# A third product unit beside the first two after each norm, square sums over all partitions, and first modulation loads in halves, in a two-layer decoder step

## What is computed

```python
def rmsnorm(x, g):
    y = x * rsqrt(mean(x * x, axis=-1) + EPS)
    return y * g
def modulated_norm(x, g, shift, scale):
    return rmsnorm(x, g) * (1 + scale) + shift
def half_ffn(x, mod, g, w_up, w_down):
    h = modulated_norm(x, g, mod[0], mod[1])
    a, b = split(h @ w_up, 2)
    return x + 0.5 * mod[2] * ((silu(a) * b) @ w_down)
# layer: half_ffn; h = modulated_norm(x); z = h @ W_in; three mixers; x += gate * W_out(...); half_ffn
```

## Time and profile before

| | us |
|---|---|
| median of three runs (3161.19 to 3166.5) | 3165.66 |
| the profiled execution | 3163.12 |
| its span, first to last instruction | 3161.5 |
| PE busy (share of the span) | 3097.9 (98%) |
| DVE, ACT, POOL busy | 1190.1, 840.8, 138.5 |
| mean granted share of the TensorE clock | 0.991 |
| DMA moved | 390.00 MB, 123 GB/s over the span |

### The profile page before, as it was taken

The page is one execution under the profiler, slowest core; times in us unless marked ns, Lnnn a source line. Parts: engine busy times, 40 slices in busy tenths (PEclk is TensorE's granted clock), DMA queues, the critical chain, the costliest instruction groups (busy, mean ns, idle before and its releaser), DMA issues. The chain is left out here.

```text
span 3161.5 us, 54219 instructions
## 1 busy us (share of the span) xinstructions
PE 3097.9 (98%) x23440; PEld 2765.0 (87%) x23440; DVE 1190.1 (38%) x2091; ACT 840.8 (27%) x1281; POOL 138.5 (4%) x269
## 2 busy tenths in 40 slices
PE   8999999999999999999999999999999999999999
PEld 6999998877777899999999999988776878899999
DVE  4333334344432344333353323442534223533333
ACT  3221224332321123212232212242324212322121
POOL 0000000000411000000000000000003120000000
PEclk9999999999999999999999999999999999999999
DMA  6444442111358432333223444312022682322212
GB/s 237 150 173 158 160 145 84 68 54 37 100 175 268 137 122 101 133 141 116 85 83 136 170 172 150 125 62 94 29 75 65 215 289 91 116 81 87 101 71 79
DMA packets 119047, 390.00 MB, mean 123 GB/s; under 512 B 12828, under 2 KB 63356, under 8 KB 100504
## 3 DMA queue, kind: packets, MB, share of 16 engines
q1 hardware_dynamic: 100608, 338.36, 30.1%
q0 software_dynamic: 14432, 34.09, 3.1%
q10 hardware_dynamic: 3768, 14.08, 1.1%
HBM read 372.79 MB, written 13.69 MB: 122 GB/s over the span
## 5 line engine op out<-in xcount | busy, mean ns | idle before, releaser
L1621 ACT ACTIVATE w_hi<-w 128x1024 fp32r<-128x1024 f32 (+2 forms) x232 | 266.0, 1147 | 1229.4 <-PE g L868 905.0
L868 PE MATMUL g<-h_hi,w_hi 128*128 128x272 f32 x2688 | 561.0, 290 | 8.4 <-ACT area L1631 4.5
L868 PE MATMUL g<-h_hi,w_lo 128*128 128x272 f32 x2688 | 556.6, 288 | 0.0
L868 PE MATMUL g<-h_lo,w_hi 128*128 128x272 f32 x2688 | 553.5, 287 | 0.0
L2200 DVE TENSOR_TENSOR w_lo<-w,w_hi 128x1024 fp32r<-128x1024 f32 (+2 forms) x232 | 309.5, 1336 | 496.0 <-ACT w_hi L1621 493.0
L868 PEld LDWEIGHTS g<-h_hi,w_hi 128*128 128x128 f32 x2688 | 422.0, 189 | 27.2 <-ACT area L1631 16.3
L868 PEld LDWEIGHTS g<-h_lo,w_hi 128*128 128x128 f32 x2688 | 421.0, 188 | 0.0
L868 PEld LDWEIGHTS g<-h_hi,w_lo 128*128 128x128 f32 x2688 | 420.4, 188 | 0.0
L868 PE MATMUL g<-h_hi,w_rest 128*128 128x272 f32 x1280 | 370.2, 289 | 0.0
L868 PE MATMUL g<-acts_hi,w_hi 128*128 128x272 f32 x1408 | 305.7, 291 | 0.1
L868 PE MATMUL g<-acts_hi,w_lo 128*128 128x272 f32 x1408 | 301.2, 288 | 0.0
(11 more groups left out here) (308 smaller groups left out, 4248.9 us busy)
## 6 DMA issues: line engine op xcount, KB each, us to landing
w<-in_w_up SPq DMA_DIRECT2D x43, 2048.0 KB, 7.8
w<-in_w_ada SPq DMA_DIRECT2D x32, 2048.0 KB, 7.9
w<-in_w_in SPq DMA_DIRECT2D x16, 2048.0 KB, 8.1
w<-in_w_down SPq DMA_DIRECT2D x16, 1536.0 KB, 6.9
w<-in_w_gate SPq DMA_DIRECT2D x48, 512.0 KB, 5.6
w<-in_w_down SPq DMA_DIRECT2D x16, 1280.0 KB, 5.7
area<-in_cache_k SPq DMA_DIRECT2D x72, 256.0 KB, 3.9
area<-in_cache_v SPq DMA_DIRECT2D x72, 256.0 KB, 4.5
```

The lines of the kernel that those rows point to most:

```text
L868: return pe.matmul(o, a, b, start=start, stop=stop, skip_group_check=True, **kw)
L1621: ac.activation(WH[i % 2][:, 0:n], W[place][:, o:o + n], ACT.Copy).then_inc(s_wh, 1)
```

## The change

- **A third unit.** From norm 1 on the third unit of the next product joins the first two (`first_units`, `first_together`). Its blocks stand in a row behind those of the first two: after block 7 of half 0 its eight blocks of half 0, and after block 7 of half 1 its eight blocks of half 1. Its result goes to the two banks `Q`, which the modulation vectors use at other times, and ACT reads it there.
- **Its weights.** Three pieces (for `ua` all four) are split ahead of the norm, at blocks 4 and 5 of the product before it, or, after the mixers, at block 5. The pieces split inside an FFN's norm are now those of units 3 and 4, and the Silu table is loaded behind block 13 of `hi_of_h`. First weights have a semaphore of their own (`s_wf`).
- **Sums on all partitions.** A half's squares are summed in four strips of 68 columns on 128 partitions, and root, reciprocal and spread work on 128 x 68. The sum for half 0 stands one block earlier in `last_pair`, that for half 1 one block later in `first_units`, and so do the spreads.
- **First loads.** Each of the pieces 1 to 3 of `w_ada` is loaded in two halves, one from SP and one from ACT. `vectors(3)` follows `vectors(2)` directly; ACT copies both rows behind block 4, and splits the two next weight pieces behind blocks 9 and 10 and loads the Silu table behind block 13.

```diff
-QT = T // 4
+QH = HALF // 4
...
+def first_together(n):
+    return 2 if n == 0 else 3
...
-        RS4, _ = take(QT, start=o_d)
+        RS4, _ = take(2, QH, start=o_d)
-        SUMS = [TB[64 * h:64 * h + 64, h, 300:300 + QT] for h in range(2)]
+        SUMS = [TB[:, h, 300:300 + QH] for h in range(2)]
...
-            sp.dma_start(WA[2], d["w_ada"][ADA_ORDER[2][1]]).then_inc(s_first[2], 16)
-            sp.wait_ge(s_first[2], 16)
+            for i in range(1, FIRST_ADA):
+                sp.dma_start(WA[i][:, 0:SLOT // 2], d["w_ada"][ADA_ORDER[i][1]][:, 0:SLOT // 2]).then_inc(s_first[i], 16)
+            sp.wait_ge(s_first[FIRST_ADA - 1], 32)
...
-                    for j in (2 * h, 2 * h + 1):
-                        last = mm(TB[32 * j:32 * j + 32, h, 300:300 + QT], ones[:, 0:32], H[:, k, j * QT:(j + 1) * QT],
+                    for j in range(4):
+                        o = h * HALF + j * QH
+                        last = mm(SUMS[h][32 * j:32 * j + 32], ones[:, 0:32], H[:, k, o:o + QH], k == 0, k == KD - 1)
...
-                mm(TB[:, h, 0:HALF], ones[r], RS[r, h * HALF:(h + 1) * HALF], True, True).then_inc(s_rs, 1)
+                mm(TB[:, h, 0:HALF], ones, RS[:, h * HALF:(h + 1) * HALF], True, True).then_inc(s_rs, 1)
...
-                            if (h, r, k) == (1, 0, 3):
+                            if (h, r, k) == (1, 0, 2):
                                 norm_sum(KD - 1, 0, (0,))
-                            if (h, r, k) == (1, 0, 7):
+                            if (h, r, k) == (1, 0, 6):
                                 spread_roots(n, 0)
...
-                    if n and q == 1:
+                    if n and q == 2:
                         norm_sum(KD - 1, 0, (1,))
-                    if n and q == 4:
+                    if n and q == 5:
                         spread_roots(n, 1)
+                    if n and k == KD - 1:
+                        for k3 in range(KD):
+                            block(2, h, k3)
+                if n:
+                    un.take()
...
-                ac.activation(RS4[r], SUMS[h], ACT.Sqrt, bias=EPSC[r, 2:3], scale=1024.0 / D).then_inc(s_rms, 1)
+                ac.activation(RS4[:, h], SUMS[h], ACT.Sqrt, bias=EPSC[:, 2:3], scale=1024.0 / D).then_inc(s_rms, 1)
...
+                    if split and q in (10, 12):
+                        split()
+                    if table and q == 13:
+                        table()
...
+                        if norm_next and m >= PAIR - 2:
+                            begin, end = ((0, 2), (2, 4 if f == 0 else 3))[m - PAIR + 2]
+                            if f == 0:
+                                hi_part(l, *[("ua", i) for i in range(begin, end)])
+                            else:
+                                first_hi(l + 1, 0, range(begin, end))
...
-            for i in range(1, FIRST_ADA, 2):
-                ac.dma_start(WA[i], d["w_ada"][ADA_ORDER[i][1]]).then_inc(s_first[i], 16)
+            for i in range(1, FIRST_ADA):
+                ac.dma_start(WA[i][:, SLOT // 2:], d["w_ada"][ADA_ORDER[i][1]][:, SLOT // 2:]).then_inc(s_first[i], 16)
...
-                link(ve.reciprocal(RS4[r], RS4[r]))
+                link(ve.reciprocal(RS4[:, h], RS4[:, h]))
```

More of the change, by code:

```diff
@@ L732, in release @@
                     splits.n += FFN_UNITS[what[2]]
+                    if what[2] == 0:
+                        together = first_together(3 * what[0] + 2 * what[1])
+                        splits.n -= together
+                        firsts.n += together
+                        sp.wait_ge(s_wf, firsts.value())
                     units.n += FFN_UNITS[what[2]]
@@ L1565, in first_norm @@
                 rows(1)
-                for q in range(KD + 1):
-                    if q == KD:
-                        rows(3)
+                for q in range(2 * KD):
                     hi_of_h(0, q)
@@ L1571, in first_norm, with norm @@
                         samples_hi(slice(0, 4))
-                    if q == 5:
+                    if q == 4:
                         rows(2)
-                for q in range(KD + 1, 2 * KD):
-                    hi_of_h(0, q)
+                        rows(3)
                     if q == 11:
                         samples_hi(slice(4, 8))
-                ac.wait_ge(s_w[0], LANDED[0])
-            def norm(n, then):
+                    if q in (9, 10):
+                        if q == 9:
+                            ac.wait_ge(s_w[0], LANDED[0])
+                        then()
+                    if q == 13:
+                        silu_table()
+            def norm(n, split=None, table=None):
                 first, second = slice(0, HALF), slice(HALF, T)
@@ L1646, in ffn @@
                     for c in range(blocks):
-                        chunk(c, half == c == 0)
+                        third = (half, c) == (0, 1) and at[0] > 4
+                        chunk(c, not half == c == 0 and not third, not half == c == 0, Q[:, :, 0:HALF] if third else None)
                         if c % 2 == 1:
@@ L1734, in _ @@
                 ffn(l, 0)
-                norm(3 * l + 1, lambda i: hi_part(l, ("ua", 2 + i)))
-                each(4, lambda i, p: ac.activation(halves(YA[:, i, :]), both(p), ACT.Gelu_apprx_tanh,
+                norm(3 * l + 1)
+                each(4, lambda i, p: ac.activation(halves(YA[:, i, :]), Q[:, :, 0:HALF] if i == 2 else both(p),
+                                                   ACT.Gelu_apprx_tanh,
                                                    bias=ZERO[:, 0:1]), l, {i: [("va", i)] for i in range(4)})
@@ L2231, in ffn @@
                     for c in range(blocks):
-                        chunk(c, c, half == c == 0)
+                        third = (half, c) == (0, 1) and at[0] > 4
+                        chunk(c, c, not half == c == 0 and not third, not half == c == 0)
                         turn_over()
@@ L2242, in ffn @@
                         turn_over()
+                        if half == 1 and norm_follows(l, f) and m >= PAIR - 2:
+                            weights_ahead(m - PAIR + 2)
                         if m % 2 == 1:
@@ L2282, in add_to_x @@
                         lo_part(l, ("out", 4 + m))
-                norm(3 * l + 2, gate, lambda r: first_lo(l, 1, r))
+                    if m == PAIR - 1:
+                        for i in range(3):
+                            first_lo(l, 1, i)
+                norm(3 * l + 2, gate, lambda nth: None)
             ve.memset(EPSC[:, 0:1], EPS)
@@ L2304, in _ @@
                 ffn(l, 0)
-                lo_part(l, ("ua", 2), ("ua", 3), *[("va", i) for i in range(4)], ("rows", 0))
+                lo_part(l, *[("va", i) for i in range(4)], ("rows", 0))
                 wait(small, 9)
```

114 lines of the change are left out of this document (55 added, 59 removed).

## The result

The changed kernel takes **3135.15 us** (median of 4 runs, 3131.3 to 3137.5). The kernel before, run beside it, takes 3163.44 (4 runs, 3161.19 to 3166.5). The ratio is 0.9909 with a 95% interval of 0.9892 to 0.9926: 28 us less, or 23 to 34. The prediction said faster, 3145.4, with a range of 3139 to 3156.

The account below looks back on a forecast made before the run. PE, busy 98% of the span, was taken as the bound. Norms -16.8, start -1.75 and clock -1.7 gave -20.3 us from the profiled 3163.12, so 3142.9; with 2.5 more for the median, 3145.4, range 3139 to 3156.

Parts of the forecast that it names:

- PE's waits in the norms cost their full length: Norms 1 to 5: PE's 26 waits, 15.4 us, cost 19.6 with overlap; 2.8 stay, so 16.8 us less.
- I take 0: Square sums: 16 instructions of half the columns for 8 cost nothing more; one half's sum may save 0.1 a norm.
- the rival by instruction: Square sums: each instruction costs 0.055 us, so 384 more cost 21 us and the gain is gone, 3166; chance 0.06.
- The floor of 25 ns a start: Square sums: matmul starts never come closer than about 25 ns, so 384 more cost 9.6 us, 3155.
- The spread over 272 columns stays as it is: Norms' chain of roots: spreading the reciprocals costs PE the same as before, so no gain was counted.
- Its idle time and about 0.16 more: PE's waits: each costs its idle time plus about 0.16 us of lost overlap between matmuls.
- Hidden weight work, landings at block 4: Products ahead of norms: earlier weight splits fit into idle time and loads land in time; price nothing.
- the slower rival: Block 4: ACT waits for late weights, holding up DVE and PE in norms 1, 3 and 4; 3172, chance 0.03.
- given back: Behind the norms: PE meets its next waits for weights or pages earlier and stands there; 3160 to 3166, chance 0.04.
- Piece 1, 2.0 us: Start: half loads on two queues remove PE's wait of 1.86 + 0.16 us for piece 1 of the first weights.
- Norm 0 behind block 0: Start: 0.2 given back by block 8, 1.1 of stretched second half, 1.65 less wait ahead of the third unit.
- The clock: Behind the wait ahead of norm 0's third unit: clock stays at 2.4 GHz, 1.7 us less, ends 0 and 1.7.

Follow-up runs that it names:

- third_behind: Changed kernel with the third unit whole behind block 15 of the first two units, PE's order alone edited: 3145.2 us, ratio 0.9946 to the kernel before.
- spread_rows: Kernel before with only the spread of the reciprocals reading 128 rows, 64 of them zeros: 3161.43 us, ratio 0.9998 to the kernel before.
- third_old_sums: Changed kernel with sums, roots, reciprocals and spreads in the old form (64 partitions for a half), at the changed places: 3137.98 us, ratio 0.993.
- loads_only: Kernel before with the first vectors' loads in halves and the new order of norm 0 alone: 3157.82 us, ratio 0.9984.
- halves_only: Kernel before with pieces 1 to 3 of w_ada loaded in two halves alone, norm 0's order as before: 3156.88 us, ratio 0.9986.
- table_behind: Changed kernel with the Silu table load of norms 2, 3 and 5 put back behind the last block of h: 3130.62 us, ratio 0.9899.
- table_all_warm: Changed kernel with the Silu table behind the last block of h in norm 0 too, plus two more products of zeros: 3131.5 us, ratio 0.9895.
- warm_more: Changed kernel with two more products of zeros at its start (26 for 24): 3136.18 us, ratio 0.9912 to the kernel before.

## Why the prediction was right in sign and too small

Of the 10.3 us between 3145.4 and 3135.15, the norms make 5.0, the start 2.6 and the rest of the program -2.2. The other 4.9 are of the step from the profiled execution to the median: I added 2.5, as in the three runs of before, but the changed kernel's median lies 2.35 below its profiled execution. So this step failed by the chance of single executions. Without it the forecast of 3142.9 against 3137.5 is still 5.4 too slow, by these steps:

- **PE's waits in the norms cost their full length.** Right. 19.6 us were forecast as lost, 2.8 of them to stay. What stayed is 4.5, with the overlap of 0.16: the table 2.4 (2.2 forecast), 1.3 in norm 1 ahead of block 6, and 0.4 ahead of block 6 in norms 2 and 5 each. third_behind shows that the third unit's place does it.
- **"I take 0" for the sums.** This is a step that failed, though its first half held: the sum of both halves has 16 instructions and takes what 8 took, 0.44, and the rival by instruction is out:

```profile
468.28 0.44 PE L880 MATMUL tb<-h,cst 128*32 128x68 f32 x16
468.65 0.40 PE L880 MATMUL g<-acts_hi,w_hi 128*128 128x272 f32 x1
```

  The floor of 25 ns a start, cited from the Trainium skill, "TensorE: Matmul & The Clock Gate", section "Wait — 56ns, not 53.3ns?", does not hold for strips side by side: 16 of them take 0.37 us to the next matmul, 23 ns each, and the four strips of a set start 7 ns apart. But a sum of one half is 0.1 us cheaper, and there are four such savings in a norm, not the one that I allowed at the lower end: 3.51 us of sums in a norm became 3.13, 0.38 each, 1.9 in five norms.
- **"The spread over 272 columns stays as it is."** Of the norms' terms this and the sums above, both put at nothing, failed most. A spread over 128 rows is 0.2 us cheaper for half 0, and 0.3 for half 1 where it now stands (in norm 4 from 2039.52 to 2040.10, 0.58 for 0.88): 2.5 in five norms. For norm 0 I even charged 0.6 for its two spreads, where (25.03 - 24.11) - (26.35 - 25.69) = 0.26 was lost. I looked at the columns and not at the rows of the tile. The Trainium skill, "TensorEngine Tiling (Array Packing)", section "Key Properties", says that a change of tiling mode drains the engine. The spread over 64 rows was such a change and the new one is not. The rows agree (0.65 to 0.36 in spread_rows, with nothing else changed on PE; and where PE has not waited ahead of it, the step into the spread is 0.22 us over 64 rows, in norm 3 of third_old_sums, and 0.13 over 128, in the same place of the changed kernel), though they do not show that the drain is the reason.
- **"Its idle time and about 0.16 more."** Mis-sized, as a wait costs a slow step behind it too: the second matmul starts 0.20 to 0.23 us after the first, for 0.125. A block of h that comes just in time has such steps with no wait in the profile, as block 13 in norm 2 of the kernel before:

```profile
1204.15 0.29 PE L868 MATMUL g<-h_hi,w_rest 128*128 128x272 f32 x1
1204.38 0.39 PE L868 MATMUL g<-h_hi,w_hi_middle 128*128 128x272 f32 x1
1204.61 0.28 PE L868 MATMUL g<-h_lo,w_hi_middle 128*128 128x272 f32 x1
```

  There were five such steps in norm 2 (three of them behind a wait) and there is one now; over the five stretches, sums and spreads left out, 26 of them lost 2.8 us and 3 lose 0.3, so 2.5 less. The prediction added up waits and could not see it.
- Together: 19.6 + 1.9 + 2.5 + 2.5 - 4.5 = 22.0, for 21.8 found.
- **Hidden weight work, landings at block 4.** Right: no wait at the end of a product ahead of a norm, so neither the slower rival nor "given back" took place.
- **Piece 1, 2.0 us.** Right: from the row behind the spreads, here as it was before, to `vectors(1)` at 29.39 it was 3.0 us; 25.03 to 26.04 is 2.0 less.

```profile
26.35 1.18 PE L868 MATMUL g<-cst 128*128 128x272 f32 x4
```

- **Norm 0 behind block 0.** The net forecast, 0.2 + 1.1 - 1.65 = -0.35, failed in both halves. Block 8 came 1.9 earlier against block 0 and not 0.2 later, since with both vectors together the wait ahead of it is 0.48 for 1.91; and from there to the third unit it is 0.7 longer, not 0.55 shorter. Net -1.2; loads_only against halves_only gives 1.3.
- **The clock.** The fall at 61 us was priced at 1.7, and from the third unit to the first turned vectors 1.5 were won. The fall at 20 us was not in the sum, and its absence in the profiled execution made 1.3. This was not foreseen, and it does not come in every execution: two of the nine profiles with the new loads have the fall. With it the start would stand at -4.8, and the profiled pair at 24.3 less, 3138.8 in place of 3137.5.

## What to carry to other kernels

When PE is the bound, moving ready work of PE into the place of its longest wait turns that wait into work: 15.3 us in five norms, with the old form of the sums. A cheaper instruction on PE gives nothing while a wait for another engine stands behind it, as the cheaper spread alone; it counts when that wait is covered, or when the same change brings the other engines' work earlier too, as the whole new form did (8.1 us without the third unit, 6.5 beside it). Price a small matmul by the tile it is put on, not only by its columns, and read PE's pitch as well as its waits. Put a table load where the engine has slack behind its last due result, not ahead of it.

## What the runs showed of the hardware

**A store waited behind the program's own code.** In norm 1 PE's wait of 1.06 us ahead of block 6 comes from DVE, which writes `h_rest` over x's place and must not do so before the last blocks of x are stored (DVE's timeline of the changed kernel):

```profile
488.29 0.91 DVE L2083 SCALAR_TENSOR_TENSOR h_rest<-area,mod,h_hi 128x272 fp32r<-128x272 f32 x2 [1.49 <-DMA out_y<-x]
```

The stores issued at 483.3 us (272 KB each) landed after 2.1 and 4.6 us, a median of 3.3; the same stores of norm 4 have 2.3, and those of norm 1 before 2.5. The data was moved by 486.3. In that moment one packet of the queue for instructions began, here in the DMA view of 486.2 to 486.4 us (packets, MB, share of 16 engines):

```profile
q8 instruction: 1, 0.02, 30.0%
```

It has 16 KB and lasts 0.96 us, from 486.28 to 487.24. The last packet of the store, 4 bytes, ends at 487.25, right behind it. In norm 4 the store's last packet ended at 2038.20, just as the code's began. The wait is there in both profiles of the changed kernel (1.06 and 1.10) and in table_behind (1.06), and shorter in table_all_warm (0.42) and warm_more (0.54, in norm 4 as well). In the second profile of the changed kernel the packet of code ran from 484.56 to 486.20, and the store's last eight packets of data followed it up to 487.24. Over all thirteen profiles the second of these stores took 3.9 to 4.6 us in the seven cases in which a 16 KB packet of code began before the store's last packet, and 2.4 to 3.2 in the other nineteen. That the packet of code is the cause is read from these times, and was not tried by an experiment.

**A longer wait and a fall of the clock go together at 20 us, but not always elsewhere**: 1.91 and 2.49 us in halves_only had no fall of the granted clock behind them, 1.92 in third_behind had one.
